# Expert loop: rows transposed two pairs ahead, next to the transpose of the hidden values

## What is computed

```
a = jnp.einsum('nd,edf->nef', h, w_gate)      # e: 32 experts, d: 1024, f: 128
b = jnp.einsum('nd,edf->nef', h, w_up)
hid = jax.nn.silu(a) * b * gates[:, :, None].astype(h.dtype)
return jnp.einsum('nef,efd->nd', hid, w_down)
```

## Time and profile before

| | |
|---|---|
| timed runs | 435.37, 439.56, 438.12 us, median 438.12 us |
| span of the profiled execution | 437.3 us |
| TensorE busy | 397.0 us, 91% |
| VectorE, ScalarE, GpSimd busy | 49%, 34%, 16% |
| DMA over the span | 109.17 MB, 250 GB/s |

### The profile page before, as it was taken

The page is one execution under the profiler, slowest core; times in us unless marked ns, Lnnn a source line. Parts: engine busy times, 40 slices in busy tenths (PEclk is TensorE's granted clock), DMA queues, the critical chain, the costliest instruction groups (busy, mean ns, idle before and its releaser), DMA issues. The chain is left out here.

```text
span 437.3 us, 6404 instructions
## 1 busy us (share of the span) xinstructions
PE 397.0 (91%) x2466; PEld 211.0 (48%) x2466; DVE 214.6 (49%) x442; ACT 150.9 (34%) x321; POOL 70.5 (16%) x59
## 2 busy tenths in 40 slices
PE   1999998999799999999989998979999999999782
PEld 1454443443244434455533557756555555554551
DVE  2968345799597465455351525741222312222276
ACT  5724122132364455454332435211222312222043
POOL 0000113444350100000000000220323223211000
PEclk9999999899899999999999999788999999999897
DMA  8981530874935133940069994899999999994384
GB/s 290 357 245 49 194 96 0 305 273 135 328 117 194 42 101 124 302 157 1 6 222 411 411 414 174 257 375 396 338 409 414 410 410 407 403 402 169 125 332 192
DMA packets 42323, 109.17 MB, mean 250 GB/s; under 512 B 7864, under 2 KB 8632, under 8 KB 42288
## 3 DMA queue, kind: packets, MB, share of 16 engines
q1 hardware_dynamic: 36000, 94.79, 58.8%
q0 software_dynamic: 5856, 12.81, 7.8%
q10 hardware_dynamic: 432, 1.11, 0.8%
HBM read 100.00 MB, written 16.94 MB: 267 GB/s over the span
## 5 line engine op out<-in xcount | busy, mean ns | idle before, releaser
L1540 PE MATMUL bank<-weights_split,tokens_split 128*128 128x512 f16 (+1 forms) x648 | 151.2, 387 | 2.1 <-DVE x L1260 1.4
L1540 PEld LDWEIGHTS bank<-weights_split,tokens_split 128*128 128x128 f16 (+1 forms) x648 | 61.8, 98 | 81.1 <-issue 12.7
L636 POOL TENSOR_TENSOR big<-big,middle 128x1536 f32<-128x1536 f32 x8 | 27.8, 3469 | 93.9 <-DMA middle<-sample_q 52.3
L1848 PE MATMUL bank<-big,tokens_split 128*64 128x256 f32 x320 | 39.0, 399 | 1.6 <-ACT tokens_split L945 1.6
L1438 DVE TENSOR_TENSOR middle<-bank,middle 128x128 f32<-128x128 f32 x16 | 4.7, 293 | 59.2 <-ACT middle L950 59.2
L1848 PEld LDWEIGHTS bank<-big,tokens_split 128*64 128x64 f32 x320 | 23.9, 143 | 13.7 <-ACT tokens_split L945 2.1
L1019 DVE SCALAR_TENSOR_TENSOR weights_split<-middle,weights_split 128x1024 f16<-128x1024 f32 x16 | 20.8, 1333 | 12.8 <-ACT weights_split L738 12.7
L1797 PE MATMUL bank<-half_consts 128*128 128x256 f16 x186 | 23.8, 294 | 2.9 <-issue 2.9
L1515 PE MATMUL bank<-ident,big 128*128 128x128 f32 (+1 forms) x92 | 14.6, 295 | 12.7 <-DVE big L1029 9.3
L670 POOL DMA_INDIRECT tokens_split<-h_rows,middle x16 | 16.3, 1018 | 59.1 <-PE bank L1837 46.0
L822 ACT ACTIVATE middle<-bank 128x128 f32<-128x128 f32 (+3 forms) x32 | 13.9, 435 | 32.0 <-PE bank L1588 31.8
(11 more groups left out here) (199 smaller groups left out, 542.8 us busy)
## 6 DMA issues: line engine op xcount, KB each, us to landing
big<-in_w_gate SPq DMA_DIRECT2D x10, 1024.0 KB, 13.8
big<-in_w_up SPq DMA_DIRECT2D x10, 1024.0 KB, 17.5
big<-in_w_down SPq DMA_DIRECT2D x10, 1024.0 KB, 15.2
middle<-in_w_in SPq DMA_DIRECT2D x16, 512.0 KB, 6.6
big<-in_cache_win_k SPq DMA_DIRECT2D x24, 256.0 KB, 3.9
middle<-in_cache_win_v SPq DMA_DIRECT2D x24, 256.0 KB, 4.6
big<-in_w_out SPq DMA_DIRECT2D x8, 512.0 KB, 8.4
big<-expert_rows SPq DMA_DIRECT2D x8, 512.0 KB, 6.9
```

The costliest lines, as they stand in the source:

```text
L636: nc.gpsimd.tensor_tensor(prod[:, :, :], kring[:, b % 2], qb[:, b % 2, :].unsqueeze(1).to_broadcast([P, NPAT, W]), ALU.mult).then_inc(prod ...
L1540: ins = T.matmul(out, (hT if rows is None else rows)[:, high_low, k if rows is None else k - 4, tokens], wg[:, place, part, k, columns], s ...
L1848: ins = T.matmul((ptb, ovb)[b][e * CAP:(e + 1) * CAP, 0:2 * FE], xT[:, b, k, e * CAP:(e + 1) * CAP], places[slot][:, 0:2, e, k * FE:(k + 1 ...
```

## The change

On TensorE the first two iterations keep turn_x(j + 1) behind gate_up (j < EARLY_ROWS = 2). From the second one on, turn_x(j + 2) follows turn_hidden(j). So iteration 1 holds turn_x(2) and turn_x(3), iterations 2 to 13 hold turn_x(4) to turn_x(15), and the last two hold none. From iteration 2 on the order is gate_up(j), down(j - 1), turn_hidden(j), turn_x(j + 2). turn_x now waits for the copies of the rows before it, as gate_up no longer stands between. On ScalarE copy_x(j + 2) moves behind copy_hidden(j), on VectorE behind copy_y(j - 1). SyncE's and GpSimd's programs are untouched, and so is the amount of work.

```diff
--- before.py
+++ after.py
@@ -56,6 +56,7 @@
 H_UP, W_UP = 16.0, 64.0
 UNDO = 1.0 / (H_UP * W_UP)
 PIECES = 4
+EARLY_ROWS = 2
 FAR = 2047.0
 
 
@@ -965,11 +966,13 @@
                 copy_x(base, 0)
                 for j in range(PAIRS):
                     silu(base + j, j % 2)
-                    if j + 1 < PAIRS:
+                    if j < EARLY_ROWS:
                         copy_x(base + (j + 1), (j + 1) % 2)
                     if j >= 1:
                         copy_y(base + (j - 1), (j - 1) % 2, isinstance(base, int) and j <= 2)
                     copy_hidden(base + j, j % 2)
+                    if EARLY_ROWS <= j + 1 < PAIRS - 1:
+                        copy_x(base + (j + 2), j % 2)
                 copy_y(base + (PAIRS - 1), 1)
 
             work(0)
@@ -1830,9 +1835,12 @@
             keep_on(30)
 
 
-            def turn_x(n, b):
+            def turn_x(n, b, first=False):
 
                 pe.wait_ge(x_landed[b], gathered(n, b))
+                if not first:
+                    pe.wait_ge(xt_a, n)
+                    pe.wait_ge(xt_d, n)
                 for k in range(KD):
                     ins = T.transpose(sbk[k // 4][:, (k % 4) * P:(k % 4 + 1) * P], xg[:, b, k * P:(k + 1) * P], ident[:, :])
                 ins.then_inc(turned, 1)
@@ -1869,10 +1877,10 @@
                 ins.then_inc(down_done, 1)
 
             def work(base):
-                turn_x(base, 0)
+                turn_x(base, 0, isinstance(base, int))
                 for j in range(PAIRS):
                     gate_up(base, j)
-                    if j + 1 < PAIRS:
+                    if j < EARLY_ROWS:
                         turn_x(base + (j + 1), (j + 1) % 2)
                     if j >= 1:
                         down(base, j - 1)
@@ -1880,6 +1888,8 @@
                         pe.wait_ge(flag_ready, 1)
                         pe.wait_ge(tab_ready, 1)
                     turn_hidden(base + j, j % 2)
+                    if EARLY_ROWS <= j + 1 < PAIRS - 1:
+                        turn_x(base + (j + 2), j % 2)
                 down(base, PAIRS - 1)
 
             work(0)
```

## The result

| | before | changed |
|---|---|---|
| median of 20 runs | 437.77 us | 440.32 us |
| lowest to highest | 433.41 to 442.06 us | 438.14 to 442.59 us |
| span of the profiled execution | 437.3 us | 439.9 us |

The ratio is 1.0084, with a 95% interval of 1.0062 to 1.0106: the changed kernel is 0.8% slower. The prediction was 439.7.

A forecast was written before the change was run, and what follows sets the result against it. The prediction took TensorE's order of work and the expert-weight stream as balanced at the loop's end. -0.1 and +1.7 (clock) gave +1.6 on the 437.3 span, 438.9; with 0.8 carried over, 439.7 us, range 435.8 to 442.0.

The forecast's parts named there:

- +1.6: Whole execution: net slowdown in us, from -0.1 at pair 15's start and +1.7 for a fall of the clock.
- the working of the loop (-0.1): Expert loop up to pair 15: its last gate and up starts 0.1 us sooner, at 396.3 instead of 396.37.
- The forms: TensorE's loop: two fewer changes between product and transpose form, 0.15 us each, shorten the period from 6.76 to 6.46 us.
- The rival in which the waits carried it: TensorE's loop: the 0.15 us belongs to semaphore waits, so the period stays 6.76; 439.2 us, chance 0.06.
- The covers: TensorE's loop: hidden transpose comes 5.3 us after gate and up starts, its input ready at 4.3; cover 1.0, no cost.
- the gathers: Row gathers in mid-loop: 2.7 us slack, no cost; rival that they bind gives about 446 us, chance 0.05.
- The one stall at turn_x(3): Behind pair 1's hidden transpose: TensorE waits once, 1.1 us, for gathered rows.
- The weights: Pair 15: TensorE ready 2.7 us sooner, but weights land about 396.3; gain 0.1 us, idle 2.6.
- the stream run dry: SyncE's loads in the loop issued 0.9 us later; taken as nothing, up to 0.9 later if the DMA queue ran dry.
- the stream theory: Posed for the experiments, on the loop's weight stream: weights land later because loads are issued later, explaining the 2.5 us.
- I take one fall: Pair 15, after 2.6 us idle: clock at 0.50 for 3.3 to 3.4 us, costing 1.7 us; chance 0.48.
- The tail: Behind pair 15 to the end: order of work and tail as in the kernel before, so no cost.

The follow-up runs named there:

- e3: Changed kernel without the loads of pair 15's gate and up weights (pair 15 uses those of pair 8, so results differ); median 435.67 us, ratio 0.9947.
- e8: Kernel before without the loads of pair 15's gate and up weights (pair 15 uses those of pair 8); median 439.57 us, ratio 1.0019.
- e1: Changed kernel with turn_x's two added waits kept only at turn_x(3); median 440.01 us, ratio 1.0009.
- e2: Changed kernel with 20 products of constants behind turn_hidden of pair 14, filling the idle time; median 437.29 us, ratio 0.9988.
- e7: Changed kernel with 60 instead of 100 products of constants behind the loop; median 438.75 us, ratio 1.0041.
- e9: Kernel of e5 with gate and up loads of the next pair issued ahead of down of this one; median 433.90 us, ratio 0.992.
- e5: Changed kernel with 12 products (24 instructions) added in TensorE's branch that isn't taken; median 437.07 us, ratio 0.9993.
- e4: Kernel before with only the two waits of turn_x added; median 439.59 us, ratio 1.0053.
- e6: Kernel before with 16 products (32 instructions) added in TensorE's branch that isn't taken; median 439.76 us, ratio 1.0058.
- e10: Kernel before with gate and up loads of the next pair issued ahead of down of this one; median 439.36 us, ratio 1.0029.

## Why the prediction was right in its number, and where it wasn't

The time (439.7 for 440.32) and the direction came out. Of the +1.6 behind them the working of the loop (-0.1) did, and that the rest came out is luck.

*The forms.* Period forecast 6.46, measured 6.45. The Trainium skill (TensorEngine Tiling (Array Packing), Key Properties) says that a change of tiling mode drains TensorE; the trace agrees, with 0.15 us for a change. The rival in which the waits carried it is out, since the new order has more waits and the shorter period.

*The covers.* The hidden transpose waits for nothing: gate and up at 389.81, transpose at 395.14, 5.3 us later as worked out, and no idle time in between. Transposes in the middle of the loop show none either, so the gathers had their slack. (The 2.95 us to the next gather is 0.25 more than its rows add up to, 1.68 + 1.02; nothing hangs on it.) The one stall at turn_x(3) was oversized: 1.1 us forecast, 0.5 to 0.65 in e1, e2, e3, e7 and e9, none in the profiles of e5 and of the changed kernel, where the rows landed as the hidden transpose ended.

*The weights.* Forecast: ready 2.7 us sooner, the weights give back 0.1, idle 2.6. Measured: 2.7 (e3 against e8), 0.3 between the profiles, idle 2.78. The later loads didn't let the stream run dry; it stayed at 407 GB/s, and the up weights of pair 15 landed 94.1 us behind the second gate_up (376.61 + 21.50 - 304.01), at 94.2 in the kernel before. So the stream theory is out. Pair 14 was closer than worked out: its weights were to land 0.7 us ahead of its start, and all profiles of the new order but those of e2 and e9 wait for them, 0.3 to 1.3 us. Without the second stall (e5) the change is worth a ratio of 0.9993, nothing that can be told, as this part of the sum had it.

*The clock.* "I take one fall" isn't borne out as put. The fall comes in two of four profiled executions, not in the changed kernel's own, and filling the idle time showed no gain over e5. With the second stall gone, e5's interval ends 1.3 us above the kernel before, short of the +1.6 of the sum. Against that stand e3's time and the mean granted clocks, by which the changed kernel's runs may well hold more such falls. How much of the 2.5 us is the clock's at pair 15 stays open.

*The tail.* The step that failed in substance is the sentence "Behind it the order is the old one, and so is the tail". The order is, but the code isn't where it was: 15 more instructions are executed (6,419 instead of 6,404), and the branch that is jumped over has grown by about as many. In the kernel before 20 constant products cover a load of instructions wholly or nearly; now 7 stand ahead of it and it stops the products for 2.82 us, the clock is low for longer, and products that do nothing but keep the clock up end 2.6 us behind the landing of the first rows that they should bridge to. e4, e5 and e6 show from three sides that the code's place costs time. The sum put this at nothing and had +1.7 for the clock instead, so that its total is near the measured one is chance.

What stays open: in e5 the position of the code is worth 3.9 us between the medians (from 2.5 above the kernel before to 1.3 below), in e6 only 1.4 and in e4 1.7, and in the changed kernel's own profile the products hold the end back by 1.0. The constant products set a floor for the end, which weighs more when the rest of an execution is quick; that may be part of it, and the clock at pair 15 another, but no run tells them apart.

## What to carry to other kernels

A loop in which two limits end together gives a gain on one of them to the other: before the work is reordered, see when the last transfer lands against when it is wanted, in more than one execution (the old order waits for it in e4 and e6 and not in the kernel before's profile), and move that transfer with it (only with its loads moved as well, and the code behind the loop shifted, was the new order 0.8% faster with the same results, in e9). Work that is there to keep a clock up stands in the queue ahead of real work, and its end belongs on the path like any other. And an edit that lengthens an engine's program can move a load of instructions into a place where it shows; a measurement of under 1% should be repeated with the code behind the edit shifted by unexecuted instructions, as e5 and e6 do, before the edit is praised or blamed.

## What the runs showed of the hardware

Code that is never executed moved the time by 0.6% and more: e6 differs from the kernel before by 32 instructions in a branch not taken and has a ratio of 1.0058 (1.0018 to 1.0097). The stall behind the jump at the end of the loop was 2.4 to 3.1 us in all these profiles. The second one came after 22 products (e1), 20 (e8, e10), 7 (changed kernel, e3, e7), 4 (e4, e6) or not at all (kernel before, e2, e5, e9), as the code was made longer or shorter. On the whole it was the shorter the longer the products ahead of it lasted: 0.31 us behind 3.23 us of them in e8, 3.01 behind 0.61 in e6. In the changed kernel a 16 KB load of instructions starts with it.

After an idle time of 2.7 to 2.9 us with dense work on either side the granted clock fell in two profiled executions of four; here such an idle time gave a chance of the lower clock, not the lower clock.
